# Stick-breaking attention of a decoder step: heads in pairs, exp taken from PSUM, page products on GpSimd

## The chip, the cores and the metric

The kernel runs on one core of a Trainium2 chip. The metric is device time in microseconds of one execution, here the median of several; less is better. The engines named below are TensorE (PE: matmuls, with PEld for its weight loads), VectorE (DVE), ScalarE (ACT), GpSimd (POOL) and SyncE (SP, which issues most DMAs). Each takes its instructions in program order; semaphores order them against one another. PSUM is the memory that TensorE writes, SBUF the other on-chip memory.

## What is computed

One inference step of a two-layer trunk for 512 prompt tokens and 8 decode tokens. Layer 0 is a convolution mixer with a dense feed-forward part, layer 1 attention with experts. The diff touches the stick-breaking attention of layer 1: 12 heads of 64 columns over the 512 tokens, and 8 decode tokens against two pages of 128 cached rows each.

```python
def _stick_breaking_block(q, k, v, bias, q_pos, k_pos):
    z = jnp.einsum('bthd,bshd->bhts', q, k, preferred_element_type=jnp.float32) * HEAD_DIM ** -0.5
    z = z + bias.astype(jnp.float32)[None, :, None, None]
    causal = k_pos[None, :] < q_pos[:, None]
    log_keep = jnp.where(causal, jax.nn.log_sigmoid(-z), 0.0)
    between = lax.cumsum(log_keep, axis=3, reverse=True) - log_keep
    w = jnp.where(causal, jnp.exp(jax.nn.log_sigmoid(z) + between), 0.0)
    return jnp.einsum('bhts,bshd->bthd', w.astype(v.dtype), v)
```

The new K and V rows (`k_prompt`, `v_prompt`, `k_sample`, `v_sample`) are outputs as well.

## The kernel before, in words

Each engine has one long instruction stream, written by hand; the order of the source is the order on the engine. Weights are split in a rounded high part and a remainder, so that matmuls in the fast 32-bit type keep precision; the same split is made of other operands where a remainder ("lo") is computed.

Ahead of the stage that matters here the projections K, V and then Q are computed, tile by tile (`M_KV`, `M_Q`). During the eight Q tiles TensorE also transposes K and V to rows (fills `TP_KV + n`, 20 of them, V first, then K), ACT and DVE copy them to `vtok`, `ktok` and `kvdec` (`kv_fill`), and when the last is copied POOL issues the four stores of the new rows, all on semaphore `kv_out` (L830 to L835). `ktok` and `kvdec` share SBUF with buffers of the attention: `wt` (weights), `zc[1]` and `sph[1]`, and the query row `qb[1]`; so their first use waits for `kv_out`.

Then comes the loop over heads, written three times. `z` of a head (128 x 1280 numbers, the causal part only) lies in three PSUM banks; two heads fit, even heads in one half, odd heads in the other.

- TensorE, iteration h: scores of head h (L2665, and a mask added by L2668), which wait until the weights of head h-2 are read out (`sb_w`); sums of head h-1 (L2681, L2684: products of the triangle `negtri` and of `negone` with the rounded part `sph`, then with the remainder `spl`), added onto z in PSUM; values of head h-2 (L2697).
- DVE: z plus bias, clamped at 40, PSUM to `zc` (L1970); the maximum of z and the logarithm, which gives the softplus `sp` (L1982); the remainder `spl` (L1991); per second head the remainder of a finished output (`mix_low`, L1675).
- ACT: exp of `zc` in place (L1240), log of 1 + that (L1242), the weights `wt` = exp of z after the sums (L1251), the rounded copy `sph` (L1255); per second head `mix_high` (L1074).

The decode tokens' page scores lie between them on DVE: in iterations 2 to 9 page n = h-2 is multiplied by the token's broadcast query (L1975, in place in `pgs`) and reduced per head (L1957, two per page, counted on `qk`). SP loads: cached K pages into `pgs`, the query row to memory and back as a broadcast (`load_query`, `qb[n % 2]`), and when page n is reduced the V page into the same place. Behind the last head a small chain treats the decode scores (`zd`, counted on `sd_step`), and the memory attention of the layer follows; its loads wait for `sb_z`, `sb_hi`, `sb_lo` and `sb_pv` of the last head.

## Time and profile before

| | us |
|---|---|
| runs of the kernel (3) | 1775.26, 1776.14, 1777.95 |
| median | 1776.14 |
| span of the profiled execution | 1771.1 |
| PE busy | 1662.0 (94%) |
| DVE busy | 958.5 (54%) |
| ACT busy | 742.6 (42%) |
| POOL busy | 540.0 (30%) |

The page of the profiled execution gives its span from the first to the last instruction; its own device time is not listed apart from it, and the median of the runs stands 5.0 us above the span. The program is a sequence of stages. In a table by stretches each engine's busy time stands with its number of instructions in brackets, then PEclk, the mean TensorE clock that was granted (1.00 is 2.4 GHz, 0.50 is 1.2 GHz), the DMA share and GB/s. In a timeline each row has a start, a time, the engine, the line, the operation, output and inputs, the count, and in square brackets the idle time of the engine ahead of it with what ended it. Rows of several instructions give the time from the first's start to the last's end. Recorded times of one engine can overlap a little.

### The profile page before, as it was taken

To read this page: it belongs to the slowest core of one execution; us is meant where nothing else is said; L and a number is where in the kernel's file an instruction comes from. 1 tells how busy PE (TensorE), PEld (TensorE's weight loads), DVE (VectorE), ACT (ScalarE), POOL (GpSimd) and SP (SyncE) were. 2 spreads that over 40 slices of the span, in tenths; PEclk is the share of its full clock that TensorE was granted. 3 is DMA by queue.
4 is the path that set the end of the run, shared out by engine and by line. 5 is a ranking of instruction groups with operands and counts; after the bars stand their busy time and mean duration, and the time that the engine had idled before them with its cause. 6 is when DMAs were issued, how large, how long until landed. Compare 5 with 4: busy or idle time off the path is not lost.

```text
span 1771.1 us, 28804 instructions
## 1 busy us (share of the span) xinstructions
PE 1662.0 (94%) x11188; PEld 1509.4 (85%) x11188; DVE 958.5 (54%) x1176; ACT 742.6 (42%) x971; POOL 540.0 (30%) x333
## 2 busy tenths in 40 slices
PE   6898888999999998989899997999999999999998
PEld 5898678999999998989566585989898998989896
DVE  6796555211111013231585625868686776868686
ACT  6355454222222123221554224445454544545454
POOL 1001232455544443332000130633241523324172
PEclk9899889999999999999898998999999999999999
DMA  6624202344455342222533415889879697987971
GB/s 203 128 78 151 71 2 71 96 136 137 148 148 190 114 153 71 84 83 72 195 128 82 137 56 142 266 239 274 221 232 257 215 298 200 282 215 235 255 250 50
DMA packets 346266, 281.94 MB, mean 159 GB/s; under 512 B 9505, under 2 KB 311117, under 8 KB 346055
## 3 DMA queue, kind: packets, MB, share of 16 engines
q1 hardware_dynamic: 324947, 251.09, 48.6%
q10 hardware_dynamic: 18084, 18.14, 3.1%
q0 software_dynamic: 3168, 11.80, 2.2%
q8 instruction: 43, 0.70, 0.2%
q14 instruction: 24, 0.20, 0.0%
HBM read 246.62 MB, written 35.10 MB: 159 GB/s over the span
## 4 chain that ended last, share of the span: by engine, by line
PE 79%; DVE 10%; ACT 4%; issue 3%; POOL 2%; DMA 1%; SPq 1%; ACTq 0%; DVEq 0%; POOLq 0%
PE ps L2351 35%; PE ps L2888 14%; PE ps L2891 6%; PE ps L2337 3%; PE ps L2338 3%; PE ps L2339 3%; PE ps L2915 2%; PE ps L2914 2%; DVE cT L1629 2%; PE ps L2490 2%; DVE wlo L1506 1%; PE ps L2319 1%; PE ps L2665 1%; DVE zc L1970 1%; PE ps L2500 1%
## 5 line engine op out<-in xcount | busy, mean ns | idle before, releaser
L2888 PE MATMUL ps<-ejx,ewh 128*128 128x384 f32 x1408 | 403.0, 360 | 3.7 <-DVE ejx L2162 1.9
L2148 DVE TENSOR_TENSOR ewl<-eraw,ewh 128x2048 fp32r<-128x2048 f32 (+1 forms) x144 | 304.1, 2112 | 153.8 <-ACT ewh L1348 153.7
L1348 ACT ACTIVATE ewh<-eraw 128x2048 fp32r<-128x2048 f32 (+1 forms) x144 | 255.2, 1773 | 257.4 <-PE ps L2891 150.3
L2891 PE MATMUL ps<-ejx,ewl 128*128 128x192 f32 x1408 | 353.1, 251 | 0.0
L2351 PE MATMUL ps<-hh,whi 128*128 128x260 f32 x1504 | 312.2, 289 | 21.7 <-DVE hl L1870 16.5
L2351 PE MATMUL ps<-hl,whi 128*128 128x260 f32 x1504 | 307.9, 287 | 0.0
L2351 PE MATMUL ps<-hh,wlo 128*128 128x260 f32 x1504 | 307.8, 287 | 0.0
L876 POOL TENSOR_TENSOR ea<-eat,ea 128x128 fp32r<-128x128 f32 x88 | 171.7, 1951 | 340.2 <-ACT ea L1406 340.0
L2888 PEld LDWEIGHTS ps<-ejx,ewh 128*128 128x128 f32 x1408 | 265.2, 188 | 7.1 <-issue 7.1
L2891 PEld LDWEIGHTS ps<-ejx,ewl 128*128 128x128 f32 x1408 | 269.9, 192 | 0.0
L2351 PEld LDWEIGHTS ps<-hh,whi 128*128 128x128 f32 x1504 | 238.2, 193 | 24.8 <-issue 16.0
L2351 PEld LDWEIGHTS ps<-hl,whi 128*128 128x128 f32 x1504 | 237.2, 193 | 0.0
L2351 PEld LDWEIGHTS ps<-hh,wlo 128*128 128x128 f32 x1504 | 237.1, 193 | 0.0
L767 POOL TENSOR_TENSOR wlo<-raw,whi 128x2048 fp32r<-128x2048 f32 x36 | 166.0, 4611 | 110.7 <-ACT whi L1206 72.8
L1903 DVE TENSOR_TENSOR tmp<-ps,rstd 128x520 f32<-128x520 f32 x44 | 30.7, 700 | 198.7 <-PE ps L2351 194.9
L761 POOL TENSOR_TENSOR wlo<-raw,whi 128x2048 fp32r<-128x2048 f32 x13 | 59.6, 4582 | 175.7 <-ACT whi L938 175.7
L2351 PE MATMUL ps<-acth,whi 128*128 128x260 f32 x352 | 72.2, 287 | 4.1 <-POOL actl L808 4.1
L2351 PE MATMUL ps<-acth,wlo 128*128 128x260 f32 x352 | 71.7, 285 | 0.0
L2351 PE MATMUL ps<-actl,whi 128*128 128x260 f32 x352 | 71.6, 285 | 0.0
L808 POOL TENSOR_TENSOR actl<-tmp,acth 128x520 f32 (+1 forms) x22 | 29.2, 1328 | 138.1 <-ACT acth L1177 138.1
L2337 PE MATMUL ps<-ewh,ea 128*128 128x512 f32 x176 | 70.3, 399 | 0.0
L2915 PE MATMUL ps<-ewl,ea 128*64 128x512 f32 x176 | 70.0, 398 | 0.0
(438 smaller groups left out, 2571.9 us busy)
## 6 DMA issues: line engine op xcount, KB each, us to landing
eraw<-in_w_gate_e SPq DMA_DIRECT2D x88, 512.0 KB, 4.8
eraw<-in_w_up_e SPq DMA_DIRECT2D x88, 512.0 KB, 6.0
eraw<-in_w_down_e SPq DMA_DIRECT2D x64, 512.0 KB, 5.9
eraw<-in_w_down_e SPq DMA_DIRECT2D x48, 256.0 KB, 2.9
xs<-zero ACTq DMA_DIRECT2D x10, 1152.0 KB, 4.8
raw<-in_w_gate_d SPq DMA_DIRECT2D x22, 512.0 KB, 4.0
raw<-in_w_up_d SPq DMA_DIRECT2D x22, 512.0 KB, 5.2
raw<-in_w_down_d SPq DMA_DIRECT2D x16, 512.0 KB, 4.5
```

The source lines that it names most:

```text
L761: e.tensor_tensor(out=wlo[:, s, :], in0=raw[:, s, :], in1=whi[:, s, :].bitcast(F32), op=ALU.subtract).then_inc(w_lo, 1)
L767: e.tensor_tensor(out=wlo[:, s, :], in0=raw[:, s, :], in1=whi[:, s, :].bitcast(F32), op=ALU.subtract).then_inc(w_lo, 1)
L876: e.tensor_tensor(out=ea[:, m, C + CB:2 * C], in0=eat[:, m % 2, 0:P], in1=ea[:, m, 0:P].bitcast(F32), op=ALU.subtract)
L1348: e.activation(ewh[:, s, 0:n], eraw[:, u % RAW, 0:n], ACT.Copy).then_inc(ew_hi, 1)
L2148: e.tensor_tensor(ewl[:, s, 0:n], eraw[:, u % RAW, 0:n], ewh[:, s, 0:n].bitcast(F32), ALU.subtract)\
L2337: e.matmul(dst, w_hi_, x_hi, start=first, stop=False, skip_group_check=check)
L2338: e.matmul(dst, w_hi_, x_lo, start=False, stop=False, skip_group_check=check)
L2339: return e.matmul(dst, w_lo_, x_hi, start=False, stop=last, skip_group_check=check)
L2351: ins = e.matmul(ps[:, 2 * q + h, 0:HALF], w, xx[:, k, h * HALF:(h + 1) * HALF], start=opens, stop=closes)
L2888: e.matmul(ps[:, q, 0:2 * C], ewh[:, s, o:o + P], ejx[:, k, :, :].rearrange("p h n -> p (h n)"), start=(k == 0), stop=(k == KD - 1), skip_ ...
L2891: ins = e.matmul(ps[:, q, C:2 * C], ewl[:, s, o:o + P], ejx[:, k, 0, :], start=False, stop=(k == KD - 1), skip_group_check=True)
L2915: ins = e.matmul(ps[0:CB, 2 + c, :], ea[:, k, P:C], wlm, start=False, stop=(k == KE - 1), skip_group_check=True)
```

## The change

The three loops over heads become loops over pairs of heads. TensorE does the scores of both heads, then the values of the two heads of the pair before, then the sums of both. ACT takes exp straight from PSUM with the bias as its argument; DVE clamps the result in SBUF at 2^57 (instead of z at 40), then log, maximum, rounded copy and remainder as before. The products of pages and queries leave DVE: POOL does them in a loop of its own behind the stores (semaphore `qp`); DVE keeps the reductions, those of two pages in each of the pairs 1 to 4, behind that pair's remainders. K is transposed to rows ahead of V, `kvdec` has K first, and POOL issues the K stores as soon as the tenth fill is copied (`k_out`), the V stores behind the twentieth (`v_out`). SP's `load_query(n + 2)` waits for the product of page n and stands ahead of the wait for that page's reductions. The decode scores' clamp, too, stands behind the exp. Some semaphores are merged (`ln_rstd` into `ln_root`, `sd_sel` into `sd_step`).

Of ACT's and DVE's loops only the new lines are shown; the lines that they replace stand in the kernel above.

```diff
-CLAMP = 40.0
+EXP_MAX = 2.0 ** 57
...
-            dst = (vtok, ktok)[w][:, i, c0:c1] if i < NT else kvdec[0:B, w, c0:c1]
+            dst = (ktok, vtok)[w][:, i, c0:c1] if i < NT else kvdec[0:B, w, c0:c1]
...
-            e.wait_ge(kv_out, 64)
+            e.wait_ge(v_out, 32)
             load_query(1)
             for n in range(B):
-                e.wait_ge(qk, 3 * n + 3)
+                if n + 2 < B:
+                    e.wait_ge(qp, n + 1)
+                    load_query(n + 2)
+                e.wait_ge(qk, 2 * n + 2)
                 load_pages(vp, n)
-                if n + 2 < B:
-                    load_query(n + 2)
...
+            copied_out(e, TP_KV + 8)
+            copied_out(e, TP_KV + 9)
+            e.dma_start(k_prompt[0].rearrange("(i p) h d -> p i (h d)", p=P), ktok[:, :, :]).then_inc(k_out, 16)
+            e.dma_start(k_sample.rearrange("b s h d -> b (s h d)"), kvdec[0:B, 0, :]).then_inc(k_out, 16)
             copied_out(e, TP_KV + 18)
             copied_out(e, TP_KV + 19)
-            e.dma_start(v_prompt[0].rearrange("(i p) h d -> p i (h d)", p=P), vtok[:, :, :]).then_inc(kv_out, 16)
-            e.dma_start(k_prompt[0].rearrange("(i p) h d -> p i (h d)", p=P), ktok[:, :, :]).then_inc(kv_out, 16)
-            e.dma_start(v_sample.rearrange("b s h d -> b (s h d)"), kvdec[0:B, 0, :]).then_inc(kv_out, 16)
-            e.dma_start(k_sample.rearrange("b s h d -> b (s h d)"), kvdec[0:B, 1, :]).then_inc(kv_out, 16)
+            e.dma_start(v_sample.rearrange("b s h d -> b (s h d)"), kvdec[0:B, 1, :]).then_inc(v_out, 16)
+            e.dma_start(v_prompt[0].rearrange("(i p) h d -> p i (h d)", p=P), vtok[:, :, :]).then_inc(v_out, 16)
             e.wait_ge(qd_out, 32)
             e.memset(wpad[0][:, :], 0.0).then_inc(wp_zero, 1)
             e.memset(wpad[1][:, :], 0.0).then_inc(wp_zero, 1)
+            for n in range(B):
+                e.wait_ge(pg_in[n], 32)
+                e.wait_ge(qb_in[n % 2], 16 * (n // 2 + 1))
+                page = pgs[:, PG_AT[n], :, :]
+                e.tensor_tensor(page, page, qb[n % 2][:, :].unsqueeze(1).to_broadcast([P, NPG, FS * P]), ALU.mult)\
+                 .then_inc(qp, 1)
...
+            def z_of(h):
+                return flat[:, 1536 * (h % 2):1536 * (h % 2) + SEG]
+            def soft_exp(h):
+                e.wait_ge(sb_z, h + 1)
+                e.activation(zc[h % 2][:, :], z_of(h), ACT.Exp, bias=bias[:, 0, h:h + 1]).then_inc(sb_e, 1)
+            def soft_log(h):
+                e.wait_ge(sb_zc, h + 1)
+                e.activation(zc[h % 2][:, :], zc[h % 2][:, :], ACT.Ln, bias=ones[:, 0:1]).then_inc(sb_l, 1)
+            def soft_high(h):
+                e.wait_ge(sb_s, h + 1)
+                e.activation(sph[h % 2][:, :], sp[h % 2][:, :], ACT.Copy).then_inc(sb_hi, 1)
+            def stick(h):
+                e.wait_ge(sb_c, h + 1)
+                if h >= 2:
+                    e.wait_ge(sb_pv, h - 1)
+                e.activation(wt[h % 2][:, :], z_of(h), ACT.Exp, bias=bias[:, 0, h:h + 1]).then_inc(sb_w, 1)
+            e.wait_ge(small_in, 64)
+            for p in range(FS):
+                soft_exp(2 * p)
+                if p == 0:
                     for n in range(2):
                         f = TP_QR + n
                         e.wait_ge(tp_done, f + 1)
                         e.activation(qrow[0:B, 512 * n:512 * n + 512], ps[0:B, 6 + f % 2, :], ACT.Copy)\
                          .then_inc(tp_free[f % 2], 1)
...
+                soft_log(2 * p)
+                if p == 0:
+                    e.wait_ge(k_out, 32)
+                soft_exp(2 * p + 1)
+                soft_high(2 * p)
+                if p == FS - 1:
+                    e.wait_ge(sd_step, SD_ZB)
+                    e.activation(zd[:, 1, :], zd[:, 0, :], ACT.Exp).then_inc(sd_step, 1)
+                soft_log(2 * p + 1)
+                soft_high(2 * p + 1)
+                if p == FS - 1:
                     e.wait_ge(sd_step, SD_ZC)
...
                     e.activation(zd[:, 1, :], zd[:, 1, :], ACT.Ln, bias=ones[:, 0:1]).then_inc(sd_step, 1)
+                if p >= 1:
+                    e.wait_ge(sb_pv, 2 * p)
+                    mix_high(p - 1, ps[:, 6 + (p - 1) % 2, :])
+                stick(2 * p)
+                stick(2 * p + 1)
...
+            def soft_low(h):
+                e.wait_ge(sb_hi, h + 1)
+                if h >= 2:
+                    e.wait_ge(sb_c, h - 1)
+                e.tensor_tensor(spl[h % 2][:, :], sp[h % 2][:, :], sph[h % 2][:, :].bitcast(F32), ALU.subtract)\
+                 .then_inc(sb_lo, 1)
+            def soft_clamp(h):
+                e.wait_ge(sb_e, h + 1)
+                e.tensor_scalar(zc[h % 2][:, :], zc[h % 2][:, :], EXP_MAX, None, ALU.min).then_inc(sb_zc, 1)
+            def soft_max(h):
+                e.wait_ge(sb_l, h + 1)
+                z = flat[:, 1536 * (h % 2):1536 * (h % 2) + SEG]
+                e.scalar_tensor_tensor(out=sp[h % 2][:, :], in0=z, scalar=bias[:, 0, h:h + 1], in1=zc[h % 2][:, :],
+                                       op0=ALU.add, op1=ALU.max).then_inc(sb_s, 1)
+            for p in range(FS):
+                soft_clamp(2 * p)
+                soft_max(2 * p)
+                soft_clamp(2 * p + 1)
+                soft_low(2 * p)
+                if p == FS - 1:
+                    e.wait_ge(sd_step, SD_E)
+                    e.tensor_scalar(zd[:, 1, :], zd[:, 1, :], EXP_MAX, None, ALU.min).then_inc(sd_step, 1)
+                soft_max(2 * p + 1)
+                soft_low(2 * p + 1)
+                if p >= 1:
+                    mix_low(p - 1, ps[:, 6 + (p - 1) % 2, :], MIX_ALL + p)
+                if 1 <= p <= B // 2:
+                    for n in (2 * p - 2, 2 * p - 1):
+                        e.wait_ge(qp, n + 1)
                         page_scores(n, 0)
...
                         page_scores(n, 1)
...
+                if p == B // 2:
                     e.wait_ge(small_in, 64)
...
+                    e.wait_ge(qk, 2 * B)
                     e.tensor_tensor(pages(zd[:, 0, :]), pages(zd[:, 0, :]), bias2, ALU.add).then_inc(sd_step, 1)
...
+                if p == FS - 1:
                     e.wait_ge(sd_step, SD_L)
                     e.tensor_tensor(zd[:, 1, :], zd[:, 0, :], zd[:, 1, :], ALU.max).then_inc(sd_step, 1)
...
+            e.wait_ge(sd_step, SD_C)
+            e.tensor_tensor(zd[:, 0, :], zd[:, 0, :], ps[:, 0, 0:192], ALU.add).then_inc(sd_step, 1)
+            mix_low(FS - 1, ps[:, 6 + (FS - 1) % 2, :], MIX_ALL + FS)
...
-            for h in range(NH + 2):
-                if h < NH:
-                    c, r = h // 2, slice(64 * (h % 2), 64 * (h % 2) + 64)
-                    z = flat[:, 1536 * (h % 2):1536 * (h % 2) + SEG]
-                    if h >= 2:
-                        e.wait_ge(sb_w, h - 1)
...
+            for p in range(FS + 1):
+                if p < FS:
+                    stick_scores(2 * p)
+                    if p == 0:
+                        for n in range(2):
+                            f = TP_QR + n
+                            fill(f, [(bank(f)[0:B, k * P:(k + 1) * P], qT[:, 4 * n + k, TP:T]) for k in range(4)])
+                    stick_scores(2 * p + 1)
+                if p == 1:
+                    copied_out(e, TP_QR)
+                    copied_out(e, TP_QR + 1)
+                if p >= 1:
+                    stick_values(2 * p - 2)
+                    if p == FS:
+                        e.wait_ge(sd_step, SD_SP)
+                        e.matmul(ps[:, 0, 0:96], negtri[:, :].bitcast(F32), zd[:, 1, 0:96], start=True, stop=False,
+                                 skip_group_check=True)
+                        e.matmul(ps[:, 0, 0:96], negone[:, :].bitcast(F32), zd[:, 1, 96:192], start=False, stop=False,
+                                 skip_group_check=True)
+                        e.matmul(ps[:, 0, 96:192], negtri[:, :].bitcast(F32), zd[:, 1, 96:192], start=False, stop=True,
+                                 skip_group_check=True).then_inc(sd_step, 1)
+                    stick_values(2 * p - 1)
+                if p < FS:
+                    stick_sums(2 * p)
+                    stick_sums(2 * p + 1)
```

The functions `soft_exp`, `soft_log`, `soft_high` and `stick` hold ACT's exp, log, rounded copy and weights; `soft_clamp`, `soft_max` and `soft_low` DVE's clamp, maximum and remainder; `stick_scores`, `stick_sums` and `stick_values` hold TensorE's three parts, whose matmuls are those of before.

DVE in the middle of the loop, one head and the start of the next before (`zc`, `sp`, `spl` are the buffers named above; the line of `hl` is `mix_low`):

```order
L1970 TENSOR_SCALAR zc_97<-ps,bias 128x1280 [waits sb_c,sb_z]
L1975 TENSOR_TENSOR pgs<-pgs,qb_106 128x1536 [waits qb_in0,pg_in2]
L1957 TENSOR_REDUCE zd<-pgs 128x12 [waits qk]
L1982 SCALAR_TENSOR_TENSOR sp_93<-ps,bias,zc_97 128x1280 [waits sb_lo,sb_l]
L1957 TENSOR_REDUCE zd<-pgs 128x12
L1991 TENSOR_TENSOR spl_102<-sp_93,sph_99 128x1280 [waits sb_hi]
L1970 TENSOR_SCALAR zc_98<-ps,bias 128x1280 [waits sb_c,sb_z]
```

and one pair now:

```order
L2001 TENSOR_SCALAR zc_97<-zc_97 128x1280 [waits sb_e]
L2007 SCALAR_TENSOR_TENSOR sp_93<-ps,bias,zc_97 128x1280 [waits sb_l]
L2001 TENSOR_SCALAR zc_98<-zc_98 128x1280 [waits sb_e]
L1995 TENSOR_TENSOR spl_102<-sp_93,sph_99 128x1280 [waits sb_c,sb_hi]
L2007 SCALAR_TENSOR_TENSOR sp_94<-ps,bias,zc_98 128x1280 [waits sb_l]
L1995 TENSOR_TENSOR spl_103<-sp_94,sph_100 128x1280 [waits sb_c,sb_hi]
```

The product has gone from DVE's row, the clamp reads and writes SBUF, and the odd head's clamp stands between the even head's maximum and remainder.

TensorE, one head before (the second and third rows of each group of matmuls left out; `wt_95` and `wt_96` are the two weight buffers):

```order
L2665 MATMUL ps<-qT,kT 128x512 [waits sb_w]
...
L2668 MATMUL ps<-future,eye 128x128 x4
L2681 MATMUL ps<-sph_99,negtri 128x512 [waits sb_hi]
...
L2681 MATMUL ps<-spl_102,negtri 128x512 [waits sb_lo]
...
L2697 MATMUL ps<-wt_96,vtok 64x512 [waits sb_w]
L2697 MATMUL ps<-wt_96,vtok 64x384
```

and one pair now:

```order
L2698 MATMUL ps<-qT,kT 128x512 [waits sb_w]
...
L2698 MATMUL ps<-qT,kT 128x512 [waits sb_w]
...
L2725 MATMUL ps<-wt_95,vtok 64x512 [waits sb_w]
...
L2725 MATMUL ps<-wt_96,vtok 64x512 [waits sb_w]
...
L2711 MATMUL ps<-sph_99,negtri 128x512 [waits sb_hi]
...
L2711 MATMUL ps<-spl_102,negtri 128x512 [waits sb_lo]
...
L2711 MATMUL ps<-sph_100,negtri 128x512 [waits sb_hi]
```

The sums of a pair now stand behind the scores of both its heads and the values of the pair before, where one head's scores stood ahead of the other's sums.

GpSimd, behind the stores, has two fills for the decode weights and then the products, which were not there:

```order
L839 DMA out<-kvdec 8x768 [waits tp_free1,tp_free0]
L840 DMA out<-vtok 128x4x768
L842 MEMSET wpad_109 128x864 [waits qd_out]
L843 MEMSET wpad_110 128x864
L848 TENSOR_TENSOR pgs<-pgs,qb_106 128x1536 [waits qb_in0,pg_in0]
L848 TENSOR_TENSOR pgs<-pgs,qb_107 128x1536 [waits qb_in1,pg_in1]
L848 TENSOR_TENSOR pgs<-pgs,qb_106 128x1536 [waits qb_in0,pg_in2]
```

Each of them waits for its page and for its query row and for nothing that DVE does in the relay.

## Rows read from the trace of the kernel before

**Rows 1.** Busy time by stretch: PE, PEld, DVE, ACT, POOL, clock, DMA

```profile
841.50:965.10 123.60, 108.06 (x472) 76.52 (x472) 86.44 (x69) 65.90 (x58) 4.21 (x6) 0.86 0.40 132
965.10:1027.30 62.20, 59.70 (x224) 30.95 (x223) 30.27 (x47) 15.88 (x47) 5.07 (x2) 0.94 0.46 137
```

**Rows 2.** Chain that ended last, in order of time, head 3

```profile
876.16 1.55 DVE zc L1970
...
877.74 1.28 ACT zc L1240
...
879.04 1.37 ACT zc L1242
...
880.43 1.56 DVE sp L1982
...
882.01 1.27 ACT sph L1255
```

**Rows 3.** Groups by line and shape, stretch 841.5 to 965.1

```profile
L1251 ACT ACTIVATE wt<-ps,bias 128x1280 f32<-128x1280 f32 x11 | 14.4, 1311 | 1.7 <-PE ps L2684 1.7
...
L1991 DVE TENSOR_TENSOR spl<-sp,sph 128x1280 fp32r<-128x1280 f32 x12 | 17.8, 1487 | 5.9 <-ACT sph L1255 5.9
L1957 DVE TENSOR_REDUCE zd<-pgs 128x12 f32<-128x768 f32 x16 | 15.2, 948 | 0.3
```

**Rows 4.** Timeline of TensorE: heads 2, 8, 10 and the last values

```profile
858.73 3.97 PE L2665 MATMUL ps<-qT,kT 64*128 64x512 f32 x8 [2.00 <-ACT wt L1251]
...
919.57 2.42 PE L2665 MATMUL ps<-qT,kT 64*128 64x512 f32 x8 [0.52 <-ACT wt L1251]
...
922.42 0.44 PE L2681 MATMUL ps<-sph,negtri 128*128 128x512 f32 x1
...
925.37 2.37 PE L2697 MATMUL ps<-wt,vtok 128*64 128x512 f32 x8
...
940.37 2.42 PE L2665 MATMUL ps<-qT,kT 64*128 64x512 f32 x8
...
970.00 2.37 PE L2697 MATMUL ps<-wt,vtok 128*64 128x512 f32 x8
```

**Rows 5.** TensorE by stretch: length, busy, clock, DMA share, GB/s

```profile
889.80:891.30 1.50, 0.04 (x1) 1.00 0.00 0
893.80:900.80 7.00, 7.00 (x26) 0.53 0.54 171
```

**Rows 6.** Groups by line and shape: one and two SBUF inputs, 192 columns

```profile
L1996 DVE TENSOR_TENSOR zd<-zd,bias 128x192 f32<-128x192 f32 x1 | 0.4, 351 | 0.0
...
L1998 DVE TENSOR_SCALAR zd<-zd 128x192 f32<-128x192 f32 x1 | 0.3, 259 | 0.0
```

**Rows 7.** Groups by line and shape: GpSimd, two 32-bit inputs

```profile
L927 POOL TENSOR_TENSOR fw<-fw,xtk 128x1024 f32<-128x1024 f32 x2 | 4.8, 2390 | 22.4 <-DVE fw L2304 22.4
```

**Rows 8.** Timeline: DVE and GpSimd at one time, two places

```profile
1757.80 2.41 POOL L927 TENSOR_TENSOR fw<-fw,xtk 128x1024 f32<-128x1024 f32 x1 [19.87 <-DVE fw L2304]
1757.94 1.28 DVE L2304 SCALAR_TENSOR_TENSOR fw<-ps,frs,tmp 128x1024 f32<-128x1024 f32 x1
1759.26 2.03 DVE L2308 TENSOR_TENSOR fw<-fw,xtk 128x1024 f32<-128x1024 f32 x1
...
1328.42 2.29 DVE L2148 TENSOR_TENSOR ewl<-eraw,ewh 128x2048 fp32r<-128x2048 f32 x1 [1.07 <-ACT ewh L1348]
1328.97 2.06 POOL L876 TENSOR_TENSOR ea<-eat,ea 128x128 fp32r<-128x128 f32 x1 [2.22 <-ACT ea L1406]
1330.63 0.61 DVE L2242 TENSOR_TENSOR eat<-eup,esg 128x192 f32<-128x192 f32 x1
```

**Rows 9.** SP's issues in the timeline, and the landing of the query rows

```profile
854.39 8.00 SPq L604 DMA_DIRECT2D pgs<-in_cache_k  x8
...
875.00 1.44 SPq L604 DMA_DIRECT2D pgs<-in_cache_v  x2
...
DMA to landing us min/median/max: 4.3/4.7/7.1
```

170 lines of the change are left out of this document (48 added, 122 removed).

## Prediction, on record before the changed kernel was run

> **What bounds the kernel now.** I read the stages first, then the chain of waits inside the one stage that the diff touches, then TensorE's timeline there. The stick-breaking stage runs from 841.5 to 965.1 us: 123.6 us, TensorE "busy" 108.1 at a mean granted clock of 0.86; the stage behind it keeps TensorE busy for 59.7 of 62.2 us [rows 1]. So what this stage gains or loses should reach the end nearly one to one: the work behind it is TensorE work in the same order, and its loads (memory K, memory V) are released by the last `sb_lo` and `sb_pv` of this stage, so they move with it.
>
> Inside the stage one head passes through a relay: DVE clamps z out of PSUM (1.55), ACT takes exp (1.28) and log (1.37), DVE the maximum (1.56), ACT the rounded copy (1.27) [rows 2], DVE the remainder (1.49), TensorE the sums, ACT the weights (1.31) [rows 3]. TensorE's own need at full clock is read from head 8: scores 919.57 to 922.42 = 2.85, both sums to 925.37 = 2.95, values 2.4, together 8.2 us per head, 16.4 per pair [rows 4]. Real progress: scores of head 2 start at 858.73, of head 10 at 940.37, so 81.6 us for eight heads, 20.4 per pair; the last head's values start at 970.00 [rows 4]. The difference is relay time, plus the clock: TensorE idles 1.5 us from 889.8, and behind that 7.0 us run at 0.53, the 1.2 GHz level [rows 5].
>
> **The change part by part.** *Pairing and the new relay.* The clamp before exp (1.55, out of PSUM) goes; exp reads PSUM directly, priced like the weights' exp, 1.31 [rows 3]. The clamp after it is a DVE TENSOR_SCALAR, SBUF to SBUF, on 1280 columns. No such row exists at that size. The nearest is the 192-column one: 0.26 us beside 0.35 for a two-input operation of the same size [rows 6]. If both have a fixed part of 0.15, the first streams 192 columns in 0.11 and the second in 0.20, about twice as fast. That gives 0.15 + 1333/2 ns = 0.83; the other bound is the two-input rate, 1.49 [rows 3]. I take 0.83, because the operation kind is the same.
>
> I write one pair down from the moment its even head's scores start, at full clock. z even 3.0; exp to 4.4; clamp to 5.2; log to 6.6; max to 8.2; rounded copy to 9.5; remainder to 11.0. Odd head: exp waits for ACT, 6.6 to 7.9; clamp behind the even max, 8.2 to 9.0; log behind the even copy, 9.5 to 10.9; max 11.0 to 12.5; copy to 13.9; remainder to 15.4; low sums to 16.9. TensorE does scores, scores, values, values until 10.4 and then the even sums, so it is never short for long: 16.9 per pair against its own 16.4, without an idle stretch of the kind that precedes the 1.2 GHz level in [rows 5].
>
> - Start: head 2's scores now wait for the sums of heads 0 and 1. From 841.5, with the extra small transposes (1.0) and half-speed sums as the kernel before shows here, 860.6 instead of 858.7: +1.9.
> - Four middle pairs: 4 x 16.9 = 67.6 for 81.6: -14.0.
> - Last pair, to the start of the last values: 16.9 + 2.4 + the decode sums and their small steps 1.1 = 20.4 for 29.6: -9.2.
>
> Together -21.3 us, if nothing disturbs the relay.
>
> *Products on GpSimd.* DVE loses its eight products; in the pair above its slack covers the sixteen reductions (0.95 each [rows 3]), so their removal is worth nothing more. GpSimd: two inputs, 1024 columns, take 2.39 [rows 7]; 1536 columns scale to 3.6, less the fixed part, 3.5 (bounds 2.8 and 3.6). Eight are 28 us. GpSimd itself is idle. The price lies elsewhere: in [rows 8] a GpSimd operation with two SBUF inputs runs from 1757.80 to 1760.21; a DVE operation that reads PSUM starts inside it and takes its ordinary 1.28; a DVE operation with two SBUF inputs starts at 1759.26 and ends at 1761.29, 1.08 after GpSimd's end. It stood still. The other way round, GpSimd waited for a DVE operation from 1328.97 to 1330.7, and DVE's next two-input one, 192 columns, took 0.61 where [rows 6] has 0.35: the one that waits gets in next.
>
> The Trainium skill says the same as a rule, and it speaks against this change: in "SBUF — State Buffer", section "SBUF: two separate sides", the port pair shared by VectorE and GpSimd is an exclusive lock for a whole instruction, taken by GpSimd or by a DVE operation with two SBUF inputs or in a 2-port mode. "VectorE: DVE Perf Modes", section "Mode 2×_2P", puts a single-source SBUF operation in that mode, so the new clamp too would take the lock. The trace agrees for the two-input case; no row here shows the clamp beside GpSimd.
>
> So the remainders (two per pair) certainly, and the clamps (two per pair) probably, stop for a running product; the maxima, with z from PSUM, do not. Where do products fall? A query row lands 4.7 us after its issue, and SP issues the two loads of a page in 1.4 us [rows 9]. SP's queue is now: wait `qp`, load query n+2, wait `qk` for page n, load V page n. So the query of page n+3 waits behind the reductions of page n, which end 1.2 us into the next pair: V pages 2.6, query 3.1, landed 7.8. In pairs 2 and 3 two products therefore start at 7.8 of the pair. First: 7.8 to 11.3; the odd clamp, ready at 8.2, runs 11.3 to 12.1. Second: 12.1 to 15.6; the even remainder, ready at 9.5, runs 15.6 to 17.1, 6.1 late. Everything behind it moves: the low sums of the odd head end near 23 instead of 16.9. TensorE idles about 5 us before the even low sums, more than the 1.5 of [rows 5], so a stretch at 1.2 GHz follows: +1.5. I count 7.6 for each of these two pairs. Pair 1 gets pages 0 and 1 early (qrow is now copied right behind the first exp, near 847 by the steps above, not behind the first relay; SP's eight page loads take 8.0 us and ended at 862.4 [rows 9], now near 856.5; the queries land near 861.5, 1 us into the pair) and page 2 behind them: 1 to 5, I take 2. Pair 4 has one product: 1.5. Pairs 0 and 5 have none. Give-back 2 x 7.6 + 2 + 1.5 = 18.7.
>
> *K rows stored first.* GpSimd issues the K store after its last weight remainder near 822, not at 842. It shares the queues with the first page loads, needed only from 861; nobody waits for it. ACT waits for `k_out` before the odd exp of pair 0 at 848, long landed. V alone goes at 842 and SP's second query waits for it. Worth nothing by itself; it keeps SP's second query, which waits for the stores, from being late. If K landed late, exp of head 1 would wait, at most 1 to 3 us. *Merged semaphores and the moved decode steps* add no instruction; the decode clamp (0.26) and its exp lie in ACT's and DVE's gaps of the last pair, or cost 0.3 each, within the 1.1 above.
>
> **Sum:** -21.3 + 18.7 = -2.6. Span 1771.1 - 2.6 = 1768.5. The median of the runs, 1776.1, stands 5.0 above the profiled span; I keep that: 1773.5.
>
> **Rivals.** *Free products.* If the products fall between DVE's port uses (4.6 us of a pair) or short ones of 2.8 do, little is given back: 1776.1 - 21.3 = 1754.8. For it: DVE needs the port for little of a pair. Against: the page chain releases products in pairs right ahead of the odd clamp and the even remainder. *Blocked and slow relay (the other side).* If every one of pairs 1 to 4 loses 7.6 and the clamp runs at 1.49 (two per pair in series, +1.3 per pair, six pairs), give-back is 30.4 + 7.9: +17 at most; with one of the two it is +9 for the four pairs alone, or +5 for the clamp alone: 1781 to 1785, 1793 the extreme. It decides as soon as more than three pairs hold two products ahead of the even remainder; the place is DVE's remainder, waiting for GpSimd. Pair 1 is where it would show first. *The gain is swallowed behind the stage.* If the memory stage waits for its 2 MB of keys instead of TensorE, less than the stage's gain arrives; with the -2.6 here that is 1775 to 1776.
>
> **How the numbers follow.** My sum, 1768 to 1781 as the alignment of products varies: 0.55. Free products, 1753 to 1758: 0.22. Blocked and slow: 0.17. Swallowed: 0.06. A measurement tells 0.2%, 3.5 us, from no change. Faster by more: the free case 0.22 and a third of my own, 0.18: 0.40. Within: 0.33. Slower: 0.17 and 0.10 of my own: 0.27. The range takes in the free case and the milder blocked ones: 1753 to 1783; the likeliest case's own is 1768 to 1781.
>
> **What would show it.** Scores of heads 2, 4, 6, 8, 10 in the timeline: 860.6, then steps of about 19, 24, 24, 18 (free: all 17). GpSimd's products near 3.5 us, longer where they meet DVE. The spread of durations of the remainders and clamps: 1.49 and 0.83 at least, up to 5 where blocked; maxima constant at 1.55. The granted clock at 0.5 for some us in the two middle pairs. A clamp minimum near 1.49 would refute its price; remainders with a constant 1.49 beside running products would refute the blocking and give 1755.

## The result, and the profile after

The changed kernel takes 1780.8 us (median of 17 runs, 1774.2 to 1784.7); beside it, on the same chip, the kernel before takes 1775.9 (17 runs, 1772.4 to 1779.5). The ratio is 1.0026, 95% interval 1.0017 to 1.0034: slower by 4.6 us, where 2.6 us faster was forecast. The time lies in the predicted range (1753 to 1783), at its slow end. The profiled span is 1777.9 us, for 1771.1 before.

The stage by pairs, cut at the moments at which the even head's scores start. Columns: length, busy time of PE, PE weight loads, VectorE, ScalarE and GpSimd with instructions in brackets, granted clock, DMA share, GB/s.

```profile
841.50:859.20 17.70, 14.72 (x73) 11.72 (x73) 8.42 (x7) 11.76 (x11) 2.88 (x4) 0.81 0.72 251
859.20:882.40 23.20, 17.63 (x82) 12.52 (x81) 15.72 (x9) 10.73 (x9) 11.42 (x3) 0.85 0.20 66
882.40:904.10 21.70, 18.55 (x82) 13.50 (x81) 16.05 (x14) 10.73 (x9) 8.32 (x2) 0.84 0.34 109
904.10:926.10 22.00, 18.14 (x82) 13.13 (x81) 15.48 (x11) 10.84 (x9) 7.44 (x2) 0.84 0.32 108
926.10:947.80 21.70, 18.30 (x82) 13.23 (x81) 16.01 (x13) 10.84 (x9) 3.48 (x1) 0.85 0.28 91
947.80:973.10 25.30, 25.30 (x95) 15.67 (x96) 9.15 (x11) 12.76 (x12) 0.58 (x1) 0.72 0.32 102
```

Pairs 1 to 4 hold 3, 2, 2 and 1 products of GpSimd, and each takes 22 to 23 us, not the 16.9 of the undisturbed relay. Pair 5 holds none; TensorE is busy through all of its 25.3 us, but at a mean clock of 0.72. TensorE's timeline, which answers to [rows 4], shows that half-rate stretch: the same eight instructions take 2.42 for head 8 and 4.63 for head 10.

```profile
926.05 2.42 PE L2698 MATMUL ps<-qT,kT 64*128 64x512 f32 x8
...
947.71 4.63 PE L2698 MATMUL ps<-qT,kT 64*128 64x512 f32 x8
...
973.04 2.37 PE L2725 MATMUL ps<-wt,vtok 128*64 128x512 f32 x8
```

The last values start at 973.04, 3.0 us later than in [rows 4]. Now the groups by line and shape of this stage (busy us, mean ns of one), the answer to [rows 3] and [rows 7]: the remainders L1995 take 2246 ns for 1487, the new clamps L2001 1532 for the 830 that were expected; the maxima L2007, which read z from PSUM, are what they were, and so are the reductions L1986.

```profile
L848 POOL TENSOR_TENSOR pgs<-pgs,qb 128x1536 f32<-128x1536 f32 x8 | 30.7, 3849 | 56.2 <-DMA qb<-qdr 56.2
L1995 DVE TENSOR_TENSOR spl<-sp,sph 128x1280 fp32r<-128x1280 f32 x12 | 27.0, 2246 | 9.3 <-ACT sph L1263 9.3
L2007 DVE SCALAR_TENSOR_TENSOR sp<-ps,bias,zc 128x1280 f32<-128x1280 f32 x12 | 18.6, 1547 | 8.6 <-ACT zc L1258 8.6
L2001 DVE TENSOR_SCALAR zc<-zc 128x1280 f32<-128x1280 f32 x12 | 18.4, 1532 | 28.0 <-ACT zc L1253 28.0
...
L1986 DVE TENSOR_REDUCE zd<-pgs 128x12 f32<-128x768 f32 x16 | 14.1, 941 | 0.0
```

The means hide where it happens. First GpSimd's timeline (start, time, count, and in brackets how long it had been idle and for what), then VectorE's clamps and remainders:

```profile
863.42 11.42 POOL L848 TENSOR_TENSOR pgs<-pgs,qb 128x1536 f32<-128x1536 f32 x3 [12.90 <-DMA qb<-qdr]
890.81 3.85 POOL L848 TENSOR_TENSOR pgs<-pgs,qb 128x1536 f32<-128x1536 f32 x1 [15.97 <-DMA qb<-qdr]
...
910.44 7.44 POOL L848 TENSOR_TENSOR pgs<-pgs,qb 128x1536 f32<-128x1536 f32 x2 [11.09 <-DMA qb<-qdr]
933.90 3.48 POOL L848 TENSOR_TENSOR pgs<-pgs,qb 128x1536 f32<-128x1536 f32 x1 [16.02 <-DMA qb<-qdr]
```

```profile
863.59 3.94 DVE L2001 TENSOR_SCALAR zc<-zc 128x1280 f32<-128x1280 f32 x1 [6.54 <-ACT zc L1253]
...
871.85 4.34 DVE L1995 TENSOR_TENSOR spl<-sp,sph 128x1280 fp32r<-128x1280 f32 x1 [0.33 <-ACT sph L1263]
...
891.94 4.08 DVE L1995 TENSOR_TENSOR spl<-sp,sph 128x1280 fp32r<-128x1280 f32 x1 [0.60 <-ACT sph L1263]
...
912.22 2.37 DVE L2001 TENSOR_SCALAR zc<-zc 128x1280 f32<-128x1280 f32 x1
914.50 4.73 DVE L1995 TENSOR_TENSOR spl<-sp,sph 128x1280 fp32r<-128x1280 f32 x1
...
934.19 3.88 DVE L2001 TENSOR_SCALAR zc<-zc 128x1280 f32<-128x1280 f32 x1
```

The first product starts at 863.42; a clamp of 0.83 us issued 0.17 us later takes 3.94. At 933.90 a single product starts, and the clamp at 934.19 takes 3.88. Six instructions, the six shown above, stood still for 1.5 to 3.2 us each and are over their undisturbed times by 16.4 us together. All lie on the relay.

Behind the stage the chain of waits runs from the last remainder through SyncE's key loads (8 issues, 10.1 us) and their landing, not through TensorE:

```profile
966.01 1.50 DVE spl L1995
...
977.49 7.76 DMA mkc<-in_cache_mem_k
985.27 1.24 DVE mkc L1715
...
1033.94 6.08 PE ps L2384 x49
```

The output projection starts at 1033.94; in the kernel before the same chain reaches it at 1027.35. So the stage's 3.0 us became 6.6. Of the 3.6 us added, 2.0 are there when VectorE starts the key product (985.27 for 980.29). The other 1.6 are TensorE's clock. With the longer wait it idles for 0.95 and then 2.00, and from 994.5 to 1001.0 it runs at a mean of 0.74; before, the longest idle time here is 1.24 and the same work runs at 1.00. The rows of the changed kernel, then of the kernel before:

```profile
991.45 1.09 PE L2544 MATMUL ps<-ident,mp 128*128 128x128 f32 x8 [0.95 <-DVE mp L1734]
994.55 2.29 PE L2533 MATMUL ps<-mkT,qT 64*128 64x256 f32 x8 [2.00 <-ACT mp L1095]
996.77 4.17 PE L2762 MATMUL ps<-pgs,wpad 128*96 128x384 f32 x8
...
989.56 1.99 PE L2500 MATMUL ps<-mkT,qT 64*128 64x256 f32 x8 [1.24 <-ACT mp L1084]
991.48 2.82 PE L2716 MATMUL ps<-pgs,wpad 128*96 128x384 f32 x8
```

### The profile page after: what moved, and what is told of

It reads as the page before. It is cut to its first block, busy times and chain, and to the rows that moved or that the text cites. A ratio compares the mean times of both kernels' runs of the same rounds, so it can differ in the third digit from the quotient of the medians.

```text
span 1777.9 us, 28796 instructions
## 1 busy us (share of the span) xinstructions
PE 1663.6 (94%) x11188; PEld 1511.1 (85%) x11188; DVE 952.9 (54%) x1168; ACT 743.0 (42%) x971; POOL 570.6 (32%) x341
## 4 chain that ended last, share of the span: by engine, by line
PE 80%; DVE 11%; ACT 4%; issue 3%; DMA 1%; POOL 1%; SPq 1%; ACTq 0%; DVEq 0%; POOLq 0%
PE ps L2384 35%; PE ps L2934 14%; PE ps L2937 6%; PE ps L2370 3%; PE ps L2371 3%; PE ps L2372 3%; PE ps L2961 2%; PE ps L2960 2%; DVE cT L1658 2%; PE ps L2523 2%; PE ps L2698 1%; DVE wlo L1535 1%; PE ps L2711 1%; PE ps L2352 1%; DVE spl L1995 1%
## 5 line engine op out<-in xcount | busy, mean ns | idle before, releaser
L2384 PE MATMUL ps<-hh,whi 128*128 128x260 f32 x1504 | 312.2, 289 | 21.7 <-DVE hl L1899 16.5
```

Source lines behind the costliest of these rows:

```text
L2384: ins = e.matmul(ps[:, 2 * q + h, 0:HALF], w, xx[:, k, h * HALF:(h + 1) * HALF], start=opens, stop=closes)
```

## Experiments

Each run is given as a ratio to the kernel before, timed on the same chip, with its 95% interval; 0.001 is 1.8 us.

### e1: products back on VectorE, pairs kept

```diff
-            for n in range(B):
-                e.wait_ge(pg_in[n], 32)
...
+                    for n in (2 * p - 2, 2 * p - 1):
+                        page_product(n)
                     for n in (2 * p - 2, 2 * p - 1):
                         e.wait_ge(qp, n + 1)
```

> The changed kernel with one part undone: DVE multiplies the pages again (two products at the end of each of the pairs 1 to 4, ahead of the four reductions); all else as changed. Theory 'lock': a GpSimd product stops DVE's two-input remainder and the clamp; without products on GpSimd the clamps stay at 0.83 and the remainders at 1.49, and only DVE's own load is left: in the slack of 5.9 us behind a pair's last remainder stand 0.7 + 2 x 1.75 + 4 x 0.95 = 8.0, so 2.1 us are lost in each of four pairs. Stage 21 - 8 = 13 shorter than before: about 1763. Theory 'pairing': the pair order itself loses (TensorE waits, then runs at 1.2 GHz), GpSimd has no part in it: then this is no faster than the changed kernel, 1781 or, with DVE loaded more, above.

Measured: 1764.8 us, 0.9929 [0.9916, 0.9943]. The remainders are at 1.49 throughout and the clamps at 0.82 but for one of 1.34 in pair 0, beside a fill by GpSimd, and the products cost VectorE 1.75 each, half of GpSimd's 3.43. The pairs take 16.9, then three times 18.2: VectorE ends its page work at 883.8, and the clamp of pair 2, whose exponential was done at 882.4, starts 1.3 us late. The whole loss of the changed kernel, and 12.6 us more, is in where the products run.

### e2: products cut to one column

GpSimd multiplies one column of 768 of each page; the output for the sampled rows is then another.

```diff
-                page = pgs[:, PG_AT[n], :, :]
+                page = pgs[:, PG_AT[n], :, 0:1]
```

> The changed kernel with each GpSimd product cut to one column of 768 per page (the rest of the page product is left out, so the decode scores are not the reference's); every wait, load and semaphore stays. Theory 'lock': nothing holds DVE for long, the whole gain of the pairing shows: 1755 (21 below before), scores of even heads every 17 us. Theory 'pairing': the pairs still take 22 us each, 1779 to 1781.

Measured: 1758.6 us, 0.9897 [0.9882, 0.9912]. TensorE's timeline has the undisturbed relay:

```profile
858.46 2.42 PE L2698 MATMUL ps<-qT,kT 64*128 64x512 f32 x8
...
875.38 2.42 PE L2698 MATMUL ps<-qT,kT 64*128 64x512 f32 x8
...
926.14 2.42 PE L2698 MATMUL ps<-qT,kT 64*128 64x512 f32 x8
...
946.37 2.37 PE L2725 MATMUL ps<-wt,vtok 128*64 128x512 f32 x8
```

16.92 us for each of four pairs, 20.23 for the last part; 16.9 and 20.4 were predicted. The stage is 23 us shorter than before, the span 17.8: about 5 us do not arrive. Again there are two parts: VectorE waits 4.42 for the keys, where it had waited 1.57, and behind that wait TensorE runs at a mean of 0.60 from 968.8 to 976.4 (e7 and e14 take up the first).

### e3: the kernel before with its products on GpSimd

> The kernel before with only the products moved to GpSimd (and the query load ahead of the wait for the reductions, as the change has it); the loop over single heads stays. Theory 'lock': some remainders go from 1.49 to 3 to 5 us, up to 8 of them; the relay of a head has little slack, so the stage gets longer by some 1 to 2 us per blocked head, less the 1.75 that DVE no longer spends: 1776 to 1786. If GpSimd does not hold DVE up: DVE loses 14 us of work that stands ahead of the maxima, and the kernel gets faster, 1768 to 1774.

Measured: 1781.2 us, 1.0024 [1.0013, 1.0035]. VectorE is rid of 14 us of products and the kernel gets slower. The timeline of both engines at one place:

```profile
877.18 3.46 POOL L845 TENSOR_TENSOR pgs<-pgs,qb 128x1536 f32<-128x1536 f32 x1 [0.30 <-DMA qb<-qdr]
877.26 4.72 DVE L1994 TENSOR_TENSOR spl<-sp,sph 128x1280 fp32r<-128x1280 f32 x1 [0.48 <-ACT sph L1263]
```

The remainder, 0.08 us late, waits out the product. It is the only one of twelve that loses a whole product; three more take 1.6 to 2.0. So a blocked remainder does not need the pairs, and taking 14 us off VectorE bought nothing. In the profiled run the stage is only 1.4 us longer than before (129.8 for 128.4); more of the loss stands behind it, where TensorE runs at a mean of 0.58 from 993.6 to 1001.7.

### e4: each product in four instructions of 192 columns

```diff
+                for q in range(4):
+                    page = pgs[:, PG_AT[n], :, 192 * q:192 * q + 192]
```

> The changed kernel with each GpSimd product cut into four instructions of 2 x 192 columns, the same work in all. Theory 'lock': the port is held for about 1.0 us at a time and the waiting engine gets in between, so a remainder or clamp loses at most about 1 us where it lost up to 3.2; two thirds of the give-back are saved: 1764 to 1770. If the loss comes from GpSimd being late with its products, or from the pairing, four smaller instructions change nothing or cost their fixed parts: 1781 to 1784.

Measured: 1771.4 us, 0.9962 [0.9948, 0.9975]. GpSimd's instructions take about 1.0, and the longest remainder 2.33 instead of 4.73. The work is the same, the holder lets go four times as often, and 11 us come back against the changed kernel by the ratios; the time is 1.4 above the range that was expected. A half-rate stretch stays in pair 2 (scores 4.63), so not all does.

### e5: products on VectorE, reductions spread over its gaps

Here `score(k)` is the k-th of the sixteen page reductions; the end of a pair keeps the two products and two of its four reductions, in pair 4 all four.

```diff
                 soft_clamp(2 * p)
+                if 2 <= p <= B // 2:
+                    score(4 * p - 6)
...
                 soft_max(2 * p + 1)
+                if 2 <= p <= B // 2:
+                    score(4 * p - 5)
```

> As e1 (products back on VectorE), but the first of a pair's page reductions are issued in the gaps of the relay, behind the clamp and behind the remainder, where VectorE waits for ScalarE or TensorE, instead of at the pair's end. Theory that the pair period in e1 (18.2 us in pairs 2 to 4, against 16.9 without page products) is VectorE's page work at the pair's end, which delays the next pair's first clamp: the periods come back to about 17 us, three pairs by 1.2 us, 1761 us against e1's 1764.8. Rival, the gaps are no idle time but stand on the relay itself, so that a reduction of 0.94 us put in one pushes everything behind it: same as e1 or up to 2 us more, 1765 to 1767.

Measured: 1760.5 us, 0.9909 [0.9895, 0.9924], 3.6 us under e1 by the ratios. All four periods are 16.9: scores of heads 2 and 4 start at 859.04 and 875.97, 16.93 apart, for 16.92 in e2. The gaps are free. The last part still takes 22.0 for e2's 20.2, because pair 4 keeps all its page work at its end and the clamp of head 10 comes late.

### e6: no clamp

VectorE's clamp of the exponential is left out, and the logarithm waits for the exponential.

> The changed kernel without VectorE's clamp of the exponential (left out altogether, the logarithm waits for the exponential). Theory of the lock: each clamp is one more two-input-port style pass on VectorE that GpSimd's product can hold up. In the changed kernel four of them took 3.94, 1.09, 2.37 and 3.88 us beside 0.82 for the others, 8 us in all on the relay, and each relay also loses its two passes of 0.82 us: 1766 to 1772 us. Rival, the blocked remainder (4 to 4.7 us) is enough by itself and whatever the clamp does not wait for the remainder or the maximum then waits for: 1777 to 1781 us.

Measured: 1768.7 us, 0.9961 [0.9947, 0.9975], as the lock theory said, but for a mixed reason, and with a wide spread (1758.3 to 1772.2). In the profiled run, its fastest, one remainder took 3.47 and four 1.9: with the clamps gone the products also fall elsewhere. It shows that blocked clamps are part of the loss, not how large a part.

### e7: e5 with the memory keys issued early

```diff
+            e.dma_start(memB.qb[:, :, :], row_broadcast(qdr[0, FS * P:D], [[D, B], [1, NMEM]])).then_inc(qm_in, 16)
+            mem_cache("cache_mem_k", 1, memB.kc, mc_in, range(6))
             e.wait_ge(sb_hi, NH)
             e.wait_ge(sb_lo, NH)
             mem_rows(1, memB)
-            e.dma_start(memB.qb[:, :, :], row_broadcast(qdr[0, FS * P:D], [[D, B], [1, NMEM]])).then_inc(qm_in, 16)
-            mem_cache("cache_mem_k", 1, memB.kc, mc_in)
+            mem_cache("cache_mem_k", 1, memB.kc, mc_in, range(6, B))
```

> e5 with one more edit: SyncE issues the broadcast of the memory query and the memory keys of six of the eight sequences right behind the release that let the queries go, and not after the last remainder of the stage. Theory that the exit of the stage runs through the last remainder, SyncE's ten microseconds of issues and the landing of the memory keys, for which VectorE waits 4 to 5 us in e1: that wait goes, 2 to 5 us less than e5, about 1757 us. Rival, the memory keys are not what is late behind the stage (TensorE's output projection is, or the earlier loads take bandwidth from the weights): within 1 us of e5.

Measured: 1757.7 us, 0.9895 [0.9880, 0.9910], the fastest kernel of this study that leaves nothing of the computation out. First e5's key product, behind a wait of 4.8 us for the keys:

```profile
962.26 1.23 DVE L1709 TENSOR_TENSOR mkc<-mkc,mqb 128x1024 f32<-128x1024 f32 x1 [4.83 <-DMA mkc<-in_cache_mem_k]
```

In e7 it starts with no wait for the keys; ahead of it VectorE now waits for TensorE, and TensorE for the memory rows, whose loads SyncE now issues behind the six key loads:

```profile
962.39 1.23 DVE L1719 TENSOR_REDUCE stm<-ps 128x4 f32<-128x1024 f32 x1 [8.55 <-PE ps L2546]
963.53 1.22 DVE L1710 TENSOR_TENSOR mkc<-mkc,mqb 128x1024 f32<-128x1024 f32 x1
```

```profile
955.50 0.66 PE L2365 MATMUL ps<-ident,mktok 128*128 128x128 f32 x4 [3.02 <-DMA mvtok<-out]
```

So one wait went and another of 3.0 us came, at a cheaper place: the output projection starts 1010.90 - 950.11 = 60.8 us behind the last values, for 64.2 in e5.

### e8: the changed kernel with V stored first again

V is transposed and copied first, K's stores are issued with V's behind the twentieth fill, and the exponential of head 1 waits for both.

```diff
-            dst = (ktok, vtok)[w][:, i, c0:c1] if i < NT else kvdec[0:B, w, c0:c1]
+            dst = (vtok, ktok)[w][:, i, c0:c1] if i < NT else kvdec[0:B, w, c0:c1]
...
                     e.wait_ge(k_out, 32)
+                    e.wait_ge(v_out, 32)
```

> The changed kernel with one part undone: V's rows are transposed and copied first again and K's rows are stored together with V's at the end, and the exponential and the queries wait for both stores. Theory that the order of K and V is worth nothing, as predicted: 1780 to 1782 us. Rival, K first lets the first exponential and the query broadcasts go earlier, and undoing it pushes GpSimd's first product and the first pair back by 1 to 4 us: 1782 to 1785 us.

Measured: 1786.6 us, 1.0048 [1.0032, 1.0064], 4 us over the changed kernel by the ratios and above both ranges. ScalarE's exponential of head 1 waits for the stores:

```profile
856.91 1.33 ACT L1252 ACTIVATE zc<-ps,bias 128x1280 f32<-128x1280 f32 x1 [5.70 <-DMA out<-kvdec]
```

Head 2's scores start 23.6 us after the stage's first, for 17.6 in the changed kernel. Without K first the pairs pay 6 us in pair 0. The order was not tried alone in the kernel before; there head 1's first use of that memory, VectorE's clamp at 853.22, waits for no store.

### e9 and e10: only some of the products

e9 cuts the products of pages 6 and 7 to one column, e10, with `n < 6` in place of `n >= 6`, those of pages 0 to 5.

```diff
+                w = 1 if n >= 6 else FS * P
+                page = pgs[:, PG_AT[n], :, 0:w]
```

> The changed kernel with GpSimd's products of pages 6 and 7, the last two, cut to one column of 768 (their output is then not the reference's); the first six stand. Theory that the 1.2 GHz stretch in pair 5 (20 us long in the changed kernel, 4.9 us lost) is set off by pair 4's blocked clamp and remainder: pair 4 comes back to 17 to 18 us from 21.7 and pair 5 runs at full clock, 8 to 9 us less, 1771 to 1773 us. Rival, the fall of the clock has nothing to do with the last products (it comes from the load of the whole stage): only pair 4's 3.5 to 4.7 us come back, 1776 to 1777 us, with scores of head 10 still at 4.6 us.

> The other way round: products of pages 0 to 5 cut to one column, only the last two at full width. Theory: pairs 1 to 3 take 16.9 us each as with all products cut (1758.6 us), pair 4 loses about 3 to 5 us to the blocked clamp and remainder and the clock falls behind it, 3 to 5 more: 1765 to 1768 us. Rival, one blocked pair alone does not bring the clock down, since it needs the idle time of the pairs before it as well: 1761 to 1763 us.

Measured: e9 1773.0 us, 0.9991 [0.9978, 1.0004], 6 us under the changed kernel by the ratios. In its profiled run pair 3, rid of page 6, takes 18.0 for 22.0, pair 4 16.9 for 21.7, and pair 5 runs at full clock, as the first theory said. But that run is the fastest of twelve (1768.5 to 1783.0), so it cannot stand for the others. The median lies at the upper end of the first theory's range; the gain over the changed kernel, 6, lies between the 8 to 9 of the first theory and the 3.5 to 4.7 of its rival. So e9 does not decide.

e10: 1763.2 us, 0.9930 [0.9917, 0.9943]. Pairs 1 and 2 take 16.9, pair 3 18.1 (a remainder of 2.63), pair 4 21.0 (a remainder of 4.07). The two products cost 5.3 us of stage and 5.9 us of time against e2. There is no half-rate stretch in pair 5, and so this is its rival's time. One product at the wrong place costs a pair 4 us.

### e11: the changed kernel with early keys

> The changed kernel with its products on GpSimd, and SyncE's broadcast of the memory query and the memory keys of six of eight sequences issued right behind the release of the last scores instead of behind the last remainder. Theory that the exit of the stage in the changed kernel runs through the last remainder, the key issues and their landing (VectorE waited 3.5 us there, 1.6 in the kernel before): 2 to 3.5 us less, 1777 to 1779 us. Rival, the work behind the stage is set by TensorE alone: 1780 to 1781 us, and the key loads beside the last pair might cost it a little.

Measured: 1772.7 us, 0.9981 [0.9966, 0.9996], 8 us under the changed kernel where 2 to 3.5 were expected, from 1766.5 to 1781.2. VectorE's wait for the keys is gone. Of the twelve runs those with a granted clock of 0.962 and more over the span take 1766.5 to 1771.2, those with 0.958 and less 1774.4 to 1781.2, and the two between them 1772.5 and 1772.8: the spread goes with how long TensorE ran at the lower level, and part of the 8 us may be this; how much is not shown.

### e12 and e15: pairs with the old first step

e1, but VectorE clamps z out of PSUM and ScalarE then takes the exponential in SBUF; in e15 the odd head's clamp also moves ahead of the even head's maximum.

```diff
-                e.activation(zc[h % 2][:, :], z_of(h), ACT.Exp, bias=bias[:, 0, h:h + 1]).then_inc(sb_e, 1)
+                e.activation(zc[h % 2][:, :], zc[h % 2][:, :], ACT.Exp).then_inc(sb_e, 1)
...
-                e.tensor_scalar(zc[h % 2][:, :], zc[h % 2][:, :], EXP_MAX, None, ALU.min).then_inc(sb_zc, 1)
+                e.tensor_scalar(zc[h % 2][:, :], z, bias[:, 0, h:h + 1], 40.0, ALU.add, ALU.min).then_inc(sb_zc, 1)
```

> e1 (pairs, products on VectorE) with the relay's old first step: VectorE clamps z out of PSUM (about 1.55 us) and then ScalarE takes the exponential in SBUF, in place of exponential from PSUM and clamp in SBUF (0.82 us). Theory that the relay's length sets the pair period: VectorE does 1.5 us more per pair and the even head's path gets 0.7 us longer, 1.5 to 2.5 us more per pair, six pairs: 1772 to 1779 us against e1's 1764.8. Rival, TensorE's 16.4 us per pair is the bound and has slack enough in pairs 0 and 5: 1766 to 1769 us.

Measured: 1792.3 us, 1.0079 [1.0065, 1.0093], 27 us over e1, far more than either theory. The timeline of pair 2:

```profile
891.33 1.54 DVE L2008 TENSOR_SCALAR zc<-ps,bias 128x1280 f32<-128x1280 f32 x1
...
897.07 1.54 DVE L2008 TENSOR_SCALAR zc<-ps,bias 128x1280 f32<-128x1280 f32 x1
898.64 1.27 ACT L1247 ACTIVATE zc<-zc 128x1280 f32<-128x1280 f32 x1 [3.07 <-DVE zc L2008]
899.82 1.25 ACT L1257 ACTIVATE sph<-sp 128x1280 fp32r<-128x1280 f32 x1
...
901.13 0.79 PE L2720 MATMUL ps<-sph,negtri 128*128 128x512 f32 x1 [5.68 <-ACT sph L1257]
```

The even head's maximum ends at 897.1, but its rounded copy stands in ScalarE's queue behind the odd head's exponential, and that behind the odd clamp: 2.7 us lost, TensorE idle for 5.7, and its next instructions at half rate. This is not the whole of it: VectorE's page work runs until 891.4, so the even clamp itself starts 2.7 us after the even scores are done (888.6).

> e12 with the odd head's clamp issued ahead of the even head's maximum instead of behind it, so that ScalarE's queue (exponential of the odd head ahead of the even head's rounded copy) does not wait for it. Theory that e12's excess is this order: the even copy and remainder come 2.3 to 2.7 us earlier than in e12, and the pair period is about 1.5 us longer than e1's (VectorE's two clamps of 1.55 for two of 0.82, its page work at the pair's end): 1772 to 1778 us. Rival, it is the page work at the pair's end that meets the longer relay, and TensorE's clock falls for the idle time all the same: 1785 us or more.

Measured: 1774.8 us, 0.9987 [0.9978, 0.9996], 16 us better than e12 by the ratios through one line's place, and in the range that was expected, though the pairs are uneven (17.7, 21.5, 19.0 and 20.2). Against e1 the exponential straight from PSUM is worth 10 us, with the page work where e1 has it.

### e13 and e14: the same products at other moments

GpSimd's product of page n also waits for the remainder of head n+2; nothing else differs from the changed kernel. e14 adds the early keys.

```diff
             for n in range(B):
+                e.wait_ge(sb_lo, n + 3)
                 e.wait_ge(pg_in[n], 32)
```

> The changed kernel with one wait more per product: GpSimd's product of page n also waits for the remainder of head n+2, so that in each of pairs 1 to 4 the first product starts at the end of the even head's remainder (VectorE then does the odd maximum, with z from PSUM) and the second at the end of the odd head's remainder (VectorE then does mix_low and reductions and has nothing for the relay for 6 us). Theory of the lock: the products now cost only the odd remainder's start by up to 0.6 us and the next clamp's by little, a period of 17.3 to 18 us, no stretch at 1.2 GHz of 20 us: 1760 to 1765 us, with a spread of the runs as small as in e1. Rival, products on GpSimd cost by something else (GpSimd's reads beside the reductions, the later V page loads): above 1770 us.

> e13 with the memory keys issued early as in e7 and e11. Theory that the exit of the stage waits for the keys whenever the stage is short, as between e5 and e7: 2.5 to 3.5 us less than e13. Rival, the gain of 8 us in e11 was of the keys and not of the spread of runs with a stretch at 1.2 GHz: 6 to 8 us less than e13.

Measured: e13 1766.4 us, 0.9937 [0.9924, 0.9950], 16 us under the changed kernel by the ratios, with one wait *added* per product. The two engines in pair 1:

```profile
870.15 1.49 DVE L1996 TENSOR_TENSOR spl<-sp,sph 128x1280 fp32r<-128x1280 f32 x1 [0.60 <-ACT sph L1264]
871.57 1.54 DVE L2008 SCALAR_TENSOR_TENSOR sp<-ps,bias,zc 128x1280 f32<-128x1280 f32 x1
871.73 3.47 POOL L849 TENSOR_TENSOR pgs<-pgs,qb 128x1536 f32<-128x1536 f32 x1 [19.78 <-DVE spl L1996]
...
874.45 2.10 DVE L1996 TENSOR_TENSOR spl<-sp,sph 128x1280 fp32r<-128x1280 f32 x1 [1.34 <-ACT sph L1264]
876.47 0.68 DVE L1705 TENSOR_TENSOR hl<-ps,hh 128x512 fp32r<-128x512 f32 x1
...
876.63 3.47 POOL L849 TENSOR_TENSOR pgs<-pgs,qb 128x1536 f32<-128x1536 f32 x1 [1.43 <-DVE spl L1996]
877.07 1.80 DVE L1987 TENSOR_REDUCE zd<-pgs 128x12 f32<-128x768 f32 x2
```

Beside the first product runs a maximum with one input from PSUM, at its ordinary 1.54; the odd remainder waits 0.6. Beside the second run `mix_low` and two reductions, at their ordinary times. The period is 17.5 in pairs 1 to 3. So of the 23 us that the full products cost in the changed kernel (its ratio against e2's), 16 are the moment at which they run, not their work or their bytes. What is left against e2 stands mostly in the last two pairs: pair 4 takes 18.8, and pair 5 25.4 for 20.2, and TensorE runs at half rate for 17 us from 929. The median lies 1.4 above the range of the first theory, the runs go from 1763.0 to 1769.7, and the "spread as small as in e1" did not come.

e14: 1759.9 us, 0.9902 [0.9887, 0.9916], 6.2 us under e13 by the ratios and 3.7 by the profiled spans; VectorE's wait for the keys falls from 3.9 to nothing. Pair 5 has the same half-rate stretch. The spans speak for the smaller figure, the medians for the larger.

## Why the prediction was wrong, step by step

**Right: the relay without disturbance.** 16.9 per pair was written down by hand, 16.92 measured in e2; the last part 20.4 against 20.2; the clamp at 0.83 (0.82 to 0.83), the exponential from PSUM at 1.31 (1.32), the product at 3.5 (3.43 to 3.47). Head 2's scores start at 859.17 where 860.6 was predicted, 1.4 on the good side.

**Right: the mechanism.** Remainders and clamps stand still for a running product, maxima do not, and e13 shows it with the same work at other moments. The Trainium skill's rule in "SBUF — State Buffer", section "SBUF: two separate sides", an exclusive lock for whole instructions, holds on all these rows. For the clamp beside GpSimd no row existed before; 3.94 and 3.88 for 0.83 now show that this one-input SBUF operation takes part too.

**Wrong: the size of the give-back in pairs 1, 4 and 5.** Changed kernel minus e2, pair by pair:

| pair | products | predicted | measured |
|---|---|---|---|
| 1 | 3 | 2 (1 to 5) | 6.3 |
| 2 | 2 | 7.6 | 4.8 |
| 3 | 2 | 7.6 | 5.0 |
| 4 | 1 | 1.5 | 4.7 |
| 5 | 0 | 0 | 5.1 |
| sum | 8 | 18.7 | 25.9 |

The step "pair 1: I take 2" failed on its own premise. The queries were to land near 861.5, so that the first product would run while VectorE was waiting. SyncE issued the first at 856.82, as worked out, but the query rows took 6.5 us to land (median of three) and not 4.7. The product started at 863.4, 0.17 us before the even clamp, and three products followed one another through the even head's half of the relay. The step "pair 4 has one product: 1.5" failed because a single product suffices: what counts is not how many fall into a pair but whether one is running when the clamp or the remainder comes up. It started 0.29 us before the odd clamp; the even remainder is queued behind that clamp on VectorE, and so the even low sums, the odd sums and the next scores all shifted. e10 confirms the size: 4 us for one product, which there holds up the even remainder. For pairs 2 and 3 the prediction was too dark by 2.6 to 2.8. In pair 2 the first product started at 890.81, 0.3 us behind the odd clamp and not ahead of it, so the clamp kept its 0.82 and the remainder got in between the two products; in pair 3 the products stopped both, but from 6.4 into the pair and not from 7.8, so that the remainder, which is ready at 9.5, had less of them to wait for. The bound stated for the slow rival, "more than three pairs hold two products ahead of the even remainder", was therefore wrong too: two pairs with two products ahead of it (1 and 3) and two with one (2 and 4) were enough.

**Wrong: the clock in pair 5.** The prediction charged half-rate stretches only to the pairs that hold the idle time, 1.5 us each in pairs 2 and 3. Pair 1 had a stretch of 7 us too. Behind pair 4's block TensorE idles for 3.4 of the 6 us from 937, and then runs at 0.50 for 20 us; from 943 on it is busy nearly all the time, through scores that take 4.63 for 2.42. That is the 5.1 us of pair 5; e13 and e14 pay the same there. What decides between a stretch of 7 us, as in pairs 1 to 3, and one of 20 stays open: e10 had an idle time of 2.3 and a stretch of 7, e13 one of 17 behind a relay that ran like that of the three pairs before.

**Wrong: "what this stage gains or loses should reach the end nearly one to one".** The prediction named the loads released by the last remainder and concluded that they move with the stage. They do, but with the last remainder and not with the last values: the remainder ends at 967.5 for 962.3, 5.2 us later, the values start 3.0 later, and VectorE, which had waited 1.6 us for the keys, waits 3.5, and 4.4 in e2, where TensorE's part of the stage had shrunk most. The rest of the loss behind the stage is TensorE's clock, which falls in that longer wait: 1.6 of the 3.6 here, 3.0 in e2. Of e2's 23 us about 5 were lost here; issuing the keys early gave e5 2.5 us back and e13 4 to 6. The rival "the gain is swallowed behind the stage" was given 0.06 and is partly true.

The sum by the measured terms: +0.4 for the start, +6.9 for the middle pairs and -4.3 for the last part make the 3.0 at the last values, and 3.6 more come behind: 6.6 of the 6.8 between the profiled spans. By the ratio of the runs it is 4.6. In the prediction's own terms, the -21.3 of the undisturbed relay was -23.0 (e2), the give-back of +18.7 was +25.9, and the nothing behind the stage was +3.6. The sign turned on the last two.

**K first, "worth nothing by itself"** was not tried by itself. e8 shows it as a condition of the pairs, worth 4 to 6 us; the prediction had put 1 to 3 on a late K, and head 1's exponential waits 5.70.
